# Squares of queries and keys summed in two rounded parts instead of one fp32 part

## The reference, cut to what matters

```python
def rms_norm(x, g):
    xf = x.astype(jnp.float32)
    y = xf * lax.rsqrt(jnp.mean(xf * xf, axis=-1, keepdims=True) + EPS)
    return (y * g.astype(jnp.float32)).astype(x.dtype)

k = rope(rms_norm(k.reshape(B, T, N_HEADS, 2, HEAD_DIM), k_norm), pos)   # shared_kv
q = rope(rms_norm(q.reshape(B, T, N_HEADS, 2, HEAD_DIM), q_norm), pos)   # diff_query
```

## Time and profile before

| | |
|---|---|
| median of 3 runs | 2439.05 us (2437.66 to 2439.99) |
| the profiled execution | 2443.61 us, span 2441.8 us |
| TensorE busy | 2340.9 us, 96% of the span |
| VectorE busy | 1686.4 us, 69% |
| ScalarE busy | 1240.0 us, 51% |
| granted TensorE clock, mean | 0.991 of full speed |

### The profile page before, as it was taken

How to read it: one execution, slowest core, us unless ns; L and a number is a source line. 1 busy time by engine, 2 the same in 40 slices (tenths; PEclk the granted TensorE clock), 3 DMA queues, 4 the chain that set the end, 5 groups by cost and what they waited for, 6 DMA issues and landing times.

```text
span 2441.8 us, 49394 instructions
## 1 busy us (share of the span) xinstructions
PE 2340.9 (96%) x20006; PEld 2040.4 (84%) x20006; DVE 1686.4 (69%) x1984; ACT 1240.0 (51%) x2236; POOL 107.8 (4%) x69
## 2 busy tenths in 40 slices
PE   5999999999998997999999999999999989899998
PEld 4999999999998996999999998999999733355555
DVE  6888788878876882555788878877667667533311
ACT  5544444444443454677555577777555345421111
POOL 3000000000000120000000000000000022300000
PEclk9999999999999998999999999999999999999999
DMA  5243444344358666324577787887889899999998
GB/s 195 84 136 105 134 130 124 105 131 136 96 157 302 212 216 219 101 92 165 178 263 251 257 287 256 289 273 260 281 309 315 304 383 422 378 369 376 391 405 302
DMA packets 383750, 573.24 MB, mean 235 GB/s; under 512 B 19577, under 2 KB 304754, under 8 KB 364274
## 3 DMA queue, kind: packets, MB, share of 16 engines
q1 hardware_dynamic: 305858, 461.55, 54.8%
q10 hardware_dynamic: 77536, 108.26, 12.3%
q0 software_dynamic: 128, 0.26, 0.0%
HBM read 509.36 MB, written 60.65 MB: 233 GB/s over the span
## 4 chain that ended last, share of the span: by engine, by line
PE 83%; DVE 6%; DMA 4%; ACT 4%; issue 2%; ACTq 0%; SPq 0%; DVEq 0%
PE psum L1080 22%; PE psum L1732 18%; PE psum L1084 11%; PE psum L1740 9%; PE psum L2438 8%; PE psum L1783 4%; PE psum L2517 4%; DMA left<-in_w_out_a_dram 2%; PE psum L2496 1%; PE psum L1748 1%; PE psum L2477 1%; DVE h_keys_turned L1674 1%; ACT w_raw L1495 1%; DMA w_raw<-in_w_in_b_dram 1%; DMA x_split_scratch<-extra_rounded 1%
## 5 line engine op out<-in xcount | busy, mean ns | idle before, releaser
L1732 PE MATMUL psum<-x_hi,w_hi 128*128 128x272 f32 x2048 | 435.0, 293 | 15.2 <-ACT w_hi L682 12.2
L1732 PE MATMUL psum<-x_lo,w_hi 128*128 128x272 f32 x2048 | 426.5, 290 | 0.0
L456 ACT ACTIVATE left_rounded<-left 128x1024 fp32r<-128x1024 f32 x280 | 295.3, 1056 | 193.2 <-PE psum L1084 173.9
L1080 PE MATMUL psum<-right_a_rounded,left_rounded 128*128 128x272 f32 x2560 | 351.2, 290 | 7.5 <-DVE right_a_rounded L775 2.8
L767 DVE TENSOR_TENSOR left_rounded<-left,left_rounded 128x1024 fp32r<-128x1024 f32 x280 | 343.2, 1228 | 21.1 <-ACT left_rounded L456 20.7
L1732 PEld LDWEIGHTS psum<-x_hi,w_hi 128*128 128x128 f32 x2048 | 322.4, 190 | 32.1 <-issue 19.6
L1080 PEld LDWEIGHTS psum<-right_a_rounded,left_rounded 128*128 128x128 f32 x2560 | 334.2, 189 | 8.7 <-issue 8.7
L1732 PEld LDWEIGHTS psum<-x_lo,w_hi 128*128 128x128 f32 x2048 | 322.2, 189 | 0.0
L1674 DVE STREAM_TRANSPOSE h_keys_turned<-h_ring 128x1024 f32<-128x1024 f32 x256 | 299.8, 1214 | 19.9 <-PE psum L1783 11.2
L1740 PE MATMUL psum<-x_hi,w_lo 128*128 128x272 f32 x2048 | 284.1, 294 | 0.0
L1080 PE MATMUL psum<-right_b_rounded,left_rounded 128*128 128x272 f32 x1920 | 267.1, 293 | 8.5 <-DVE work L794 8.4
(11 more groups left out here) (253 smaller groups left out, 2737.0 us busy)
## 6 DMA issues: line engine op xcount, KB each, us to landing
h_ring<-in_cache_k_dram SPq DMA_DIRECT2D x256, 512.0 KB, 6.4
ring<-in_cache_v_dram SPq DMA_DIRECT2D x128, 1024.0 KB, 8.2
left<-in_w_in_a_dram SPq DMA_DIRECT2D x128, 512.0 KB, 4.1
w_raw<-in_w_kv_dram SPq DMA_DIRECT2D x16, 2048.0 KB, 12.7
w_raw<-in_w_in_b_dram SPq DMA_DIRECT2D x15, 2048.0 KB, 9.1
left<-in_w_out_a_dram SPq DMA_DIRECT2D x32, 512.0 KB, 5.6
wo_raw<-in_w_out_b_dram SPq DMA_DIRECT2D x32, 512.0 KB, 8.2
ring<-in_w_out_b_dram SPq DMA_DIRECT2D x16, 1024.0 KB, 6.5
```

Of the source, the lines that this page charges most:

```text
L456: act.activation(arena.left_high(q), arena.left(LEFT[mm], n), ACT.Copy).then_inc(hi_ready, 1)
L1080: pe.matmul(to, wh[:, k * P:(k + 1) * P], arena.right(RIGHT[mm], low)[:, k * GT:(k + 1) * GT], start=(mm in OPENS and k == 0 and low == 0) ...
L1732: pe.matmul(psum[n % 2][:, g, 0:GT], m.WH[n % 2][:, k * P:(k + 1) * P], x[:, k * T + g * GT:k * T + (g + 1) * GT], start=(k == 0 and x is ...
```

## The change

The square is computed twice by ScalarE: once in fp32 (into `r`), and once with an fp32r output (into `sq_high`, which is the memory of `tile`). VectorE subtracts the second from the first, into an fp32r view of `r` (`sq_low`), behind `split_lo(n + 1)`. TensorE sums both parts with a rounded matrix of ones, four fp32r matmuls where two fp32 ones stood, and does it between the halves of `lo_part` and no longer ahead of it. The second square waits for the DMA of the block that was in `tile` before, and for its transposes. In the convolution layer the semaphore `cg_scaled` is folded into `gate_step`, which now counts four steps a round.

```diff
-GATES = 3
+GATES = 4
...
-            pool.wait_ge(cg_scaled, EDGE)
...
-                    act.wait_ge(gate_step, GATES * i + 1)
+                    act.wait_ge(gate_step, GATES * i + 2)
...
-                dve.wait_ge(cg_scaled, i + 1)
+                dve.wait_ge(gate_step, GATES * i + 1)
...
-                    scaled(cg, rs2).then_inc(cg_scaled, 1)
+                    scaled(cg, rs2).then_inc(gate_step, 1)
...
-        tile = [sb(f"tile{s}", [P, T]) for s in range(2)]
+        with nc.sbuf_tensor("h_tile_rounded", [P, 2 * T], F32R) as tile_rounded:
+            pass
+        both_tiles = sb("tile", [P, 2 * T])
+        tile, sq_high = ([t[:, s * T:(s + 1) * T] for s in range(2)] for t in (both_tiles, tile_rounded))
+        sq_low = [m.WORK_ROUNDED[:, (2 + s) * T:(3 + s) * T] for s in range(2)]
...
                 if normed(n):
                     act.activation(r[s][:, :], plain[s][:, :], ACT.Square).then_inc(sq_ready, 1)
+                    after(act, scratch_out[s], 16 * kept_in_slot(n))
+                    after(act, turned, turns_before(n - 1))
+                    act.activation(sq_high[s], plain[s][:, :], ACT.Square).then_inc(sq_ready, 1)
...
+            def split_square(n):
+
+                if normed(n):
+                    s = n % 2
+                    dve.wait_ge(sq_ready, 2 * norms_before(n) + 2)
+                    dve.tensor_tensor(sq_low[s], r[s][:, :], sq_high[s].bitcast(F32), ALU.subtract).then_inc(sq_split, 1)
...
             dve.wait_ge(tables_in, 32)
+            dve.tensor_copy(m.ONES_ROUNDED[:, :], m.ONES[:, :])
             split_lo(1)
...
                     split_lo(n + 1)
+                if n >= 1:
+                    split_square(n - 1)
...
-                    pe.wait_ge(sq_ready, norms_before(n) + 1)
-                    for g in range(G):
-                        last = pe.matmul(psum[n % 2][:, g, 0:GT], m.ONES[:, :], r[n % 2][:, g * GT:(g + 1) * GT],
-                                         start=True, stop=True)
+                    pe.wait_ge(sq_split, norms_before(n) + 1)
+                    for part in (sq_high[n % 2], sq_low[n % 2]):
+                        for g in range(G):
+                            last = pe.matmul(psum[n % 2][:, g, 0:GT], m.ONES_ROUNDED[:, :], part[:, g * GT:(g + 1) * GT],
+                                             start=(part is sq_high[n % 2]), stop=(part is sq_low[n % 2]), skip_group_check=True)
...
-                if n >= 1:
-                    sum_squares(n - 1)
                 after(pe, lo_ready, n)
                 if n == 0:
                     pe.wait_ge(one.q_low, 1)
                 lo_part(n, first)
+                if n >= 1:
+                    sum_squares(n - 1)
```

More of the change, by code:

```diff
@@ L142, in memory @@
     m.ONES = sb("ones", [P, P])
+    m.ONES_ROUNDED = sb("ones_rounded", [P, P], F32R)
     m.EPSC = sb("eps", [P, 1])
@@ L278, in seven_products @@
         act_took, dve_took = sem("act_took"), sem("dve_took")
-        cg_scaled, us_step, u_ready = sem("cg_scaled"), sem("us_step"), sem("u_ready")
+        us_step, u_ready = sem("us_step"), sem("u_ready")
         lu_ready, lr_ready, lr_out = sem("lu_ready"), sem("lr_ready"), sem("lr_out")
@@ L854, in make_y @@
             def make_y(i):
-                dve.wait_ge(gate_step, GATES * i + 3)
+                dve.wait_ge(gate_step, GATES * i + 4)
                 dve.tensor_tensor(b2, b2, cg, ALU.mult).then_inc(y_ready, 1)
@@ L934, in conv_extras @@
                     if mm == 3:
-                        dve.wait_ge(gate_step, GATES * i + 2)
+                        dve.wait_ge(gate_step, GATES * i + 3)
                         scaled(cg, rs).then_inc(gate_step, 1)
@@ L1370, in project_and_score @@
         block_done, evacuated = sem("block_done"), sem("evacuated")
-        sq_ready, summed, r_step, tile_ready = sem("sq_ready"), sem("summed"), sem("r_step"), sem("tile_ready")
+        sq_ready, sq_split, summed, r_step, tile_ready = sem("sq_ready"), sem("sq_split"), sem("summed"), sem("r_step"), sem("tile_ready")
         turned, rows_ready, granted, dve_step = sem("turned"), sem("rows_ready"), m.granted, sem("dve_step")
```

## The result

The changed kernel takes 2488.84 us (median of 4 runs, 2485.6 to 2491.75) against 2439.12 before: a ratio of 1.0201, interval 1.0189 to 1.0214, or 49.7 us more. The forecast was 2484. The profiled execution took 2491.75 us, with a span of 2490.0 and a mean granted clock of 0.982 against 0.991.

The account below looks back on a forecast made before the run. TensorE alone was taken to set the time, other engines' work being free unless late. Net q passes +19.1, k passes +12.3 and clock falls +13.5 made +45 us, 2484 us against the median; range 2463 to 2500.

Parts of the forecast that it names:

- The saving: Normed passes: four fp32r matmuls take 0.50 us where the fp32 sum cost 0.91, 0.41 us less a pass.
- The chain of 15.7 us: Odd q passes: sum to sum through Ln, scaling, squares, splits and subtraction, against TensorE's 12.56; waits of 3.15 us.
- Pass 1: First normed q pass: its sum now waits for `split_lo(2)` and the subtraction, so pass 2 starts 3.3 us later.
- Pass 1 had its fall already: Clock term: no new fall of TensorE's clock was counted for pass 1; each fall was priced at 1.5 us.
- k passes: Waits in passes 33, 36, 39, 41, 45 and 47, 18.9 us net, less 6.6 saved: +12.3 us.
- The clock: TensorE's clock falls behind 9 of 12 new waits, 1.5 us each: +13.5 us; all 12 would be +18.
- What costs nothing: Zero for `gate_step`, GpSimd's dropped wait and the copy of the ones; the second square's old-tile wait was zero too.
- The wait for the old tile: ScalarE's second square waits for the old tile: zero; upper end 3 us later in each of eight even passes.
- the later place: Sum moved half a pass: in pass 36 both copies and `split_lo` move with Ln, 1.6 us later.
- Outside the two stages: Rest of the kernel, outside both stages: the span stays unchanged.
- The rival with the parts ready when asked: Sums never wait, the change only saves: 2426 us, needing a chain under 12.56 in the q passes; chance 0.06.
- the rival with more than the forecast: Tile DMA 3 us late in eight even k passes, or late key transposes: 24 on top, 2508 us; chance 0.13.

Follow-up runs that it names:

- experiment 4: Changed kernel without the subtraction, sum back ahead of the low weights' part and taking the rounded squares twice: 2430.54 us, ratio 0.9966.
- Experiment 1: Changed kernel with VectorE's subtraction ahead of the weight split instead of behind it: 2440.24 us, ratio 1.0003 to the kernel before.
- experiment 2: Changed kernel with the sum back ahead of the low weights' part, subtraction still behind the weight split: 2496.75 us, ratio 1.0231.
- Experiment 3: Changed kernel with throwaway matmuls on TensorE ahead of its wait in the odd q passes: 2480.41 us, ratio 1.0165.
- experiment 7: Changed kernel with the subtraction ahead of the weight split and the weights' scaling behind the next odd round's squares: 2467.29 us, ratio 1.0116.
- experiment 5: Kernel before with only its fp32 sum moved between the halves of `lo_part`, no second square or subtraction: 2448.17 us, ratio 1.0032.
- experiment 9: Changed kernel with the subtraction ahead of the weight split and the sum in its old place: 2432.93 us, ratio 0.9965.
- experiment 10: The kernel of experiment 7 with memory of its own for the rounded squares of even blocks: 2445.02 us, ratio 1.0027 to the kernel before.
- experiment 6: Changed kernel with each pair's scaling moved behind the next odd round's squares, subtraction still behind the weight split: 2523.22 us, ratio 1.035.

## Why the prediction was right

Of the sum's terms, in its order:

- **The saving** of 0.41 us a pass: passes with no wait and no fall of the clock, in them or running into them, are 0.39 to 0.44 us shorter in the changed kernel, and experiment 4 has the matmuls without the waits and is 0.41 us a pass faster in the q passes. Shown.
- **The chain of 15.7 us** in odd q passes: 15.70 between the sums at 1017.63 and 1033.33. Seven waits of 2.96 to 2.98 us as idle time stood for 3.15 counted from start to start. Experiment 1 takes one link out (the weight split ahead of the subtraction) and all seven vanish; experiment 2 moves the sum and none changes. Shown by both.
- **Pass 1:** the wait was 4.4 us, not the 6.9 that the sum implies, since the scaling of the weights began at 961.51 us, 1.8 earlier than in the kernel before. The fall of the clock, which now came inside pass 1, took 2.1 us. From the start of pass 1 to that of pass 2 it is 3.2 us more than before, where 3.3 stood: two errors that cancel. "Pass 1 had its fall already" was wrong as well: the 1.5 us that the fall had cost in pass 2 are gone from there, and pass 2 is 1.8 us shorter and not 0.4.
- **k passes:** waits of 1.20 (1.2 forecast), 5.81 (5.9), 2.56 and 2.55 (2.7), 4.25 and 4.25 (4.0), and one of 0.48 in pass 35 that was not foreseen. The tables of the code gave the right passes.
- **The clock,** 13.5 us from 9 falls of 1.5. In the q passes four of the seven waits brought one, 1.5 us each. In the k passes the three long waits did and the two of 2.55 us did not. From the sum to the start of the next pass it is 7.1, 6.8 and 5.7 us in passes 36, 41 and 47, and 4.2 in passes 34, 37, 38 and 40, which wait for nothing: 2.9, 2.5 and 1.5 us lost. That makes 6.1 + 6.9 = 13.0, nearly the 13.5 but from other parts: seven falls for nine, two of them longer, so the near match is in part luck. To it come the 2.1 us in pass 1, less the 1.5 that it cost before. Experiment 3 shows that the falls in the q passes are due to the idle time, and measures them from the first q sum on at 6.7 us. The rule of the Trainium skill, page "TensorE: Matmul & The Clock Gate", Part 1, that the default state is throttled and activity releases it, agrees with that; taken for each wait it would have given 18 us, and waits of the very same length here fell on both sides.
- **What costs nothing:** two terms were set at zero and are so only in this arrangement. The wait for the old tile was 1.3 us in all in the changed kernel's q passes, but 18.2 in experiment 7. And the later place, which I priced through pass 36 alone, costs 6 us in the k passes by itself (experiment 5: the k sums span 262.1 for 256.1 us). In the changed kernel it is not seen apart. There the waits are for the subtraction, but for the 2.20 us for keys in pass 36, and the later place even gains in passes 1 and 33 (experiment 2).

Outside the two stages the changed kernel's span is 2.9 us longer, where I had said unchanged. The last part varies over the kernels run, which are all alike there: from the start of pass 49 to the end it is 757.9 to 762.3 us. The changed kernel has the longest of all, the one before has 758.6. The time at the half clock in this part goes along with it: 10 to 20 us over the kernels, 20.5 in the changed one and 13.7 in the one before. By that, some 3.4 of the 3.8 us go with falls of the clock in the profiled execution; what brought them was not tried. The median lies 4.8 us above the forecast, and single runs of the changed kernel spread by 6 us.

The rival with the parts ready when asked is what experiments 1 and 9 built in the q passes. It needed the chain under 12.56 us, and one exchange of two calls on VectorE does it. Its 2426 us was not reached by either (2440.24 and 2432.93), since the k passes keep waits for keys and for pass 36. Of the rival with more than the forecast, no wait for a k tile is seen in the changed kernel, and in its k passes only one for keys, the 2.20 us in pass 36.

## What to carry to other kernels

An operand that an engine makes behind another one's work inherits all that the other waits for: put the short instruction that TensorE will ask for ahead of the long one whose input is late. Moving the consumer later hides nothing when what it releases feeds the next round of the same chain (it hid 2 us only where a chain starts, in passes 1 and 33), and it can make the work behind it late; compare the chain from one sum to the next with TensorE's own time between them, not the lateness within a pass. And a wait that shows as zero in a trace is worth the distance to its cover: ask what stands between, before that is moved.

## What the runs showed of the hardware

In the changed kernel, waits of 2.96 to 2.98 us lowered TensorE's clock in four cases of seven, 2.55 and 2.56 in none of two, and those of 3.6 us and more each time. The length does not decide it alone: a wait of 2.20 us for keys in pass 36 left the clock at 1.00 there and lowered it in experiments 1, 5 and 10. Ahead of pass 1 an idle stretch of 2.04 us lowered it, where one of 2.84 us at the same matmuls had not in the kernel before:

```profile
946.70 3.79 PE L1119 MATMUL psum<-extra,ones 128*128 128x272 f32 x8 [2.04 <-POOL extra L393]
...
948.00:950.00 2.00, 2.00 (x7) 0.50 0.00 0
```

One fall cost 1.5 us in most cases and 2.5 and 2.9 us in two. In the changed kernel the 256 KB store of a q tile landed in 2.1 us by the median and in 8.6 us at worst, and one such late store held up ScalarE by 6 us where the tile's memory was wanted early (experiments 6 and 7).
